# Down projection with paired products: four separate products in one row ahead of the last four groups

## The chip, the cores and the metric

The kernel runs on one core of a Trainium2 chip. The metric is the device time of one execution in microseconds (us). The engines are TensorE (PE, matrix products), VectorE (DVE), ScalarE (ACT), GpSimd (POOL) and SyncE (SP), which here only issues DMAs. Each engine runs its own instructions in order and waits for the others by semaphores.

## What is computed

A model of 256 tokens and width 2048: a gMLP block, a stick-breaking attention block, then a block with mLSTM and MoBA attention and an FFN. The change lies in that last FFN, all in fp32:

```
x2 = rmsnorm(x, norm_ffn_pre)
u  = square(relu(x2 @ w_up))        # 256x2048 @ 2048x8192
y  = u @ w_down                     # 256x8192 @ 8192x2048
x  = x + rmsnorm(y, norm_ffn_post)
```

## The kernel before, in words

**Three products for one.** A weight block is loaded to `stage`. ACT rounds it to a high half (`wh`, line 657), DVE makes the low half `wl` = block - `wh` (line 1173), and PE runs low x high, high x high and high x low in place of one fp32 product (lines 2125 to 2127). The tokens are split likewise into `yth` and `ytl`. The unit of the order is a *group*: one 512 KB weight load (256 x 512), split once, 12 matmuls for two token halves and two rows of 128. `home` (built at lines 255 to 262) lists all 935 groups in the order in which PE runs them. `wh` and `wl` hold 5 groups, so ACT splits group j once PE has ended group j - 5 (signal `used`). `where[...]` and `end(...)` give positions in this list.

**Order by slots.** Each engine's program is written out by hand. `slot(n)` in ACT's and DVE's programs means: first do all high (low) halves up to position n + 3; in SP's: first issue all loads whose buffer comes free up to n + 3. What stands behind a `slot` is done after that, in order.

**The FFN** runs in four quarters q of the hidden width. In each, `up` has four chunks c of 512 columns. ACT takes relu and square of a finished chunk (1122, 1125), DVE turns it (`turn_chunk`, 1234), SP moves it into `ytl` with four DMAs (479), ACT makes its high half (`up_high`, which calls `chunk_high`, 685) and DVE its low half (`chunk_low`, 1222). Then `down` multiplies these 2048 rows by four chunks of 512 output columns, summed in `dacc`.

**Pairs.** Two neighbouring chunks of `down`, (q, 0) with (q, 1) and (q, 2) with (q, 3), make a *pair*; there are 7, numbered 0 to 6 (at q = 3 only the first). For their first 512 rows, a 2 x 2 product of blocks is done with seven half products instead of eight, as in Strassen's and Winograd's method. A half product is a group of 6 matmuls (lines 2188 to 2190). P2, P3 and P4 are added into the banks of the pair's own chunks. The four *separate* products P1, P5, P6 and P7 each have a bank of their own, 4 to 7. The weights of a pair are four blocks, b11, b12, b21 and b22. P1 uses b11 itself. P5 uses t1 = b12 - b11 (line 1185), P6 uses t2 = b22 - t1 (1190), P7 uses t3 = b22 - b12 (1192), and P4 uses t4 = b21 - t1 (1195). DVE makes each of them in place, in `operand`, right behind the low half of the group before in the chain (t1 behind P1's, t2 behind P5's, t3 behind P6's), and ACT's high half of the product waits for it.

**The pair around PE.** The separate products stand in the list among the last four groups of the unit before the pair: at pairs 0, 2, 4 and 6 that unit is `up` (q, 3), at pairs 1, 3 and 5 it is the pair (q, 0), whose last four groups are k = 12 and 14 of both chunks. `apart` (ACT) copies P1's bank to SBUF (1101) and P5's bank to `rowb` (`fifth`, 1108). `together` (DVE) makes u2 = P6 + P1 (1957), u3 = P7 + u2 (1961), v = u2 + P5 (1963) and w = u3 + P5 (1965). `early` (DVE, 1974) adds the four results to `dacc` from q = 1 on. `down_evac` adds a finished chunk's banks.

For q = 2 the positions are: `up` (2, 3) begins at 822 and ends at 834 (`end`, the position behind its last group); P1 is 826.

Of the kernel before, what the change touches and what calls it, by code (L numbers as in the profile page):

```python
# [11 lines left out]
ALU = mybir.AluOpType  # L12
ACT = mybir.ActivationFunctionType
# [17 lines left out]
P1, P5, P6, P7, P2, P3, P4 = range(7)  # L31
# [105 lines left out]
def _program(nc, A, out, ctx):  # L137
    at = [((nc.sbuf_base + 511) // 512) * 512]

    def sb(name, shape, dt=F32, offset=None):  # L140
        size = int(np.prod(shape[1:])) * (2 if dt == BF16 else 4)
        where = at[0] if offset is None else offset
        if offset is None:
            at[0] += (size + 31) // 32 * 32
            assert at[0] <= nc.sbuf_usable_end, (name, at[0])
        t = nc.alloc_sbuf_tensor_at("t_" + name, shape, dt, offset=where)
        return t[tuple(slice(None) for _ in shape)], where
# [11 lines left out]
    rowb, _ = sb("rowb", [128, 2, 512])  # L159
# [33 lines left out]
    banks = [ctx.enter_context(nc.psum_tensor(f"bank{i}", [128, 512], F32))[:, :] for i in range(8)]  # L193
# [21 lines left out]
    used = signal("used")  # L215
# [7 lines left out]
    act = signal("act")  # L223
# [4 lines left out]
    vec = signal("vec")  # L228
# [6 lines left out]
    pairs = halved_pairs()  # L235
# [19 lines left out]
    home = []  # L255
    for u, (_, own) in enumerate(units):
        m = units[u + 1][0] if u + 1 < len(units) else None
        for n, group in enumerate(own):
            ahead = n - len(own) + 4
            if m is not None and ahead >= 0:  # L260
                home.append((m, ahead))
            home.append(group)
    N = len(home)
    where = {h: j for j, h in enumerate(home)}
    first = {chunk[0]: where[chunk[0], 4 if chunk[0] in pair_of else 0] for chunk in chunks}
# [51 lines left out]
    def end(*name):  # L317
        return max(j for j, (x, k) in enumerate(home) if x == name) + 1
# [16 lines left out]
    def cols(c):  # L335
        return slice(512 * c, 512 * c + 512)
# [35 lines left out]
    sum_l, sum_h = mtl[:, 0:4, :], mtl[:, 4:8, :]  # L372
    sum_raw = vreg[:, 4096:5120].rearrange("p (f s) -> p f s", f=4)
    added = vreg[:, 6144:8192].rearrange("p (f s) -> p f s", f=4)
    fifth = rowb[:, 0, :]

    def g8(j):
        return gsm[:, j, :]
# [194 lines left out]
    def gpsimd(e):  # L573
# [62 lines left out]
                e.tensor_tensor(h, h, d, ALU.add).then_inc(*pool("x3", c, i))  # L636

        for c in range(4):
            e.wait_ge(*(vec.at("dr", c - 2, 1) if c >= 2 else vec.at("w", "pair", len(pairs) - 1)))
            load_row(c, A["norm_ffn_post_2"][:, cols(c)], "ffn", c)  # L640


    def scalar(e):
# [16 lines left out]
        def slot(n):  # L660
            highs(n + 3)
# [423 lines left out]
                e.wait_ge(*(pool.at("x3", c, i) if c >= 2 else vec.at("x3", c, i)))  # L1085
                squares(hres[:, i, cols(c)], ssq2[:, i, c:c + 1], "x3", c, i)
        def up_high(q, c):
            slot(end("up", q, c) + 4)
            chunk_high(yth, ytl, c, 1.0, "up", q, c)
            if c == 0:  # L1090
                slot(end("up", q, c) + 5)
                e.wait_ge(*vec.at("sums", q))
                e.activation(sum_h, sum_raw, ACT.Copy).then_inc(*xhi("sums", q))

        def apart(m):

            slot(where[m, P1] + 1)
            e.wait_ge(*used.at(where[m, P1]))
            if m and pairs[m - 1][0][1]:
                e.wait_ge(*vec.at("early", m - 1, 0))  # L1100
            e.activation(quarters(m)[0], banks[4], ACT.Copy).then_inc(*act("first", m))
            slot(where[m, P5] + 1)
            e.wait_ge(*used.at(where[m, P5]))
            if m:
                e.wait_ge(*vec.at("w", "pair", m - 1))
            else:
                e.wait_ge(*vec.at("mixed", 2))
            e.activation(fifth, banks[5], ACT.Copy).then_inc(*act("fifth", m))

        e.wait_ge(*vec.at("sF"))  # L1110
        for q in range(4):
            for c in range(4):
# [48 lines left out]
    def vector(e):  # L1161
# [35 lines left out]
        def slot(n):  # L1197
            lows(n + 3)
# [142 lines left out]
        for p, n in ((0, 37), (1, 40)):  # L1341
# [3 lines left out]
            for q in (2 * p, 2 * p + 1):  # L1345
                w = wst[:, 4 * q:4 * q + 4, :]
# [24 lines left out]
        for h in range(2):  # L1371
            for c in range(4 * h, 4 * h + 4):
# [11 lines left out]
                for i in range(2):  # L1384
                    v = v_tile(c, i)
# [551 lines left out]
        def up_turn(q, c):  # L1937
            slot(end("up", q, c) + 1)
            e.wait_ge(*act.at("squared", q, c))
            turn_chunk(lambda i: buf[c % 2][:, i, :], flat[zt_buf[c]], "up", q, c)  # L1940
            slot(end("up", q, c) + 4)
            if c == 0:
                sums(q)
            chunk_low(yth, ytl, c, 1.0, "up", q, c)
            if c == 0:
                slot(end("up", q, c) + 6)
                e.wait_ge(*xhi.at("sums", q))
                e.tensor_tensor(sum_l, sum_raw, sum_h.bitcast(F32), ALU.subtract).then_inc(*xlo("sums", q))

        def together(m):  # L1950

            _, q, c = pairs[m][0]
            one, three_, two, four_ = quarters(m)
            slot(where[m, P6] + 1)
            e.wait_ge(*used.at(where[m, P6]))
            e.wait_ge(*act.at("first", m))
            e.tensor_tensor(two, banks[6], one, ALU.add).then_inc(*vec("u2", m))
            slot(where[m, P7] + 1)
            e.wait_ge(*used.at(where[m, P7]))
            e.wait_ge(*vec.at("u2", m))  # L1960
            e.tensor_tensor(three_, banks[7], two, ALU.add).then_inc(*vec("u3", m))
            e.wait_ge(*act.at("fifth", m))
            e.tensor_tensor(two, two, fifth, ALU.add).then_inc(*vec("v", "pair", m))
            e.wait_ge(*vec.at("u3", m))
            e.tensor_tensor(four_, three_, fifth, ALU.add).then_inc(*vec("w", "pair", m))

        def early(m):
            _, q, c = pairs[m][0]
            if q:
                slot(where[m, P7] + 3)  # L1970
                e.wait_ge(*vec.at("w", "pair", m))
                for n in range(2):
                    d = dacc[:, :, cols(c + n)]
                    e.tensor_tensor(d, d, added[:, 2 * n:2 * n + 2, :], ALU.add).then_inc(*vec("early", m, n))  # L1974

        def down_evac(q, c):
            slot(end("down", q, c))
            e.wait_ge(*used.at(end("down", q, c) - 1))
            if q == 3:
                e.wait_ge(*row_in[c % 2].at("ffn", c))  # L1980
            for i in range(2):
                d, p = dacc[:, i, cols(c)], accs("down", q, c)[i]
                e.tensor_tensor(d, d, p, ALU.add).then_inc(*vec("d", q, c, i))
                if q == 3:
                    e.wait_ge(*vec.at("d", 3, c, i))
                    e.tensor_tensor(buf[c][:, i, :], d, rowb[:, c % 2, :], ALU.mult).then_inc(*vec("dr", c, i))

        for q in range(4):
            for c in range(3):
                up_turn(q, c)  # L1990
            together(first_of["down", q, 0])
            up_turn(q, 3)
            early(first_of["down", q, 0])
            down_evac(q, 0)
            if ("down", q, 2) in first_of:
                together(first_of["down", q, 2])
            down_evac(q, 1)
            if ("down", q, 2) in first_of:
                early(first_of["down", q, 2])
            for c in range(2, 3 if q == 3 else 4):  # L2000
                down_evac(q, c)
# [115 lines left out]
    def tensor(e):  # L2117
        count = {"group": 0}
        free = {}
# [47 lines left out]
        def halved(m, f, j):  # L2167

            a, b = pairs[m]
            bank = {P1: banks[4], P5: banks[5], P6: banks[6], P7: banks[7], P2: accs(*a)[0], P3: accs(*b)[0],  # L2170
                    P4: accs(*a)[1]}[f]
            if f <= P7:
                bank_of(4 + f)
                free[4 + f] = (act.at("first", m), act.at("fifth", m), vec.at("u2", m), vec.at("u3", m))[f]
            if f in (P1, P2):
                e.wait_ge(*arrival(("down", a[1], 0), 0))
            elif f == P5:
                e.wait_ge(*xlo.at("sums", a[1]))
            for n in range(2):
                h, l = {P1: (tokens(yth, 2 * n, 0), tokens(ytl, 2 * n, 0)),  # L2180
                        P2: (tokens(yth, 2 * n + 1, 0), tokens(ytl, 2 * n + 1, 0)),
                        P4: (tokens(yth, 2 * n + 1, 1), tokens(ytl, 2 * n + 1, 1)),
                        P5: (tokens(sum_h, 0, n), tokens(sum_l, 0, n)),
                        P6: (tokens(sum_h, 1, n), tokens(sum_l, 1, n)),
                        P7: (tokens(sum_h, 2, n), tokens(sum_l, 2, n)),
                        P3: (tokens(sum_h, 3, n), tokens(sum_l, 3, n))}[f]
                w_h, w_l = wh[:, j % N_SPLIT, n, :], wl[:, j % N_SPLIT, n, :]
                e.matmul(bank, h, w_l, start=n == 0 and f <= P7, stop=False)  # L2188
                e.matmul(bank, h, w_h, start=False, stop=False)  # L2189
                last = e.matmul(bank, l, w_h, start=False, stop=n == 1 and f <= P7)  # L2190
            return last
# [361 lines left out]
```

## Time and profile before

| what | us |
|---|---|
| median of 3 runs | 2572.11 (2571.88 to 2573.97) |
| the profiled execution, its own time | 2571.94 |
| span of that execution, first to last instruction | 2570.2 |
| PE matmul busy | 2560.8 |
| DVE busy | 1674.4 |
| ACT busy | 1275.5 |
| POOL busy | 34.8 |

The times of one execution come from the hardware profiler. Busy time counts an engine's instructions; waits are not busy. PE's matmuls are pipelined and their ends are modelled, so that one record reaches over the start of the next. Lines (L1173) are lines of the kernel before. The FFN fills the stretch from about 1.87 ms to the end.

### The profile page before, as it was taken

The page shows a single profiled execution, that of the slowest core. Times are in us where ns is not written, and L with a number is a line of the kernel's source. Part 1 is how long each engine was busy: PE and PEld are TensorE (multiplying, and loading weights), DVE is VectorE, ACT ScalarE, POOL GpSimd, SP SyncE. Part 2 cuts the span into 40 slices and gives each one's busy share as a digit, 9 for nine tenths or more (in the row PEclk, how much of TensorE's full clock was granted, in tenths as well). Part 3 has the DMA queues.
Part 4 walks back from the last instruction along what each step waited for, and adds up shares of the span by engine and source line. Part 5 has one row for each costly group of instructions (what it writes and reads, how often), then busy time and mean ns, then how long its engine had stood idle before and what let it go on. Part 6 is the DMA issues. An engine that isn't in the chain of part 4 may idle for free.

```text
span 2570.2 us, 29334 instructions
## 1 busy us (share of the span) xinstructions
PE 2560.8 (100%) x11461; PEld 2122.5 (83%) x11461; DVE 1674.4 (65%) x1949; ACT 1275.5 (50%) x1534; POOL 34.8 (1%) x56
## 2 busy tenths in 40 slices
PE   9999999999999999999999999999999999999999
PEld 8888888888888888888888888888888888888887
DVE  5646565566666566676866876555577668577676
ACT  6554443444545555455444444444465455464453
POOL 1000000000000000000000000000020000000000
PEclk9999999999999999999999999999999999999999
DMA  8767776676777777777565777666666667666674
GB/s 284 205 185 209 208 204 194 198 206 198 215 217 199 212 202 202 219 228 221 162 195 168 217 219 211 201 201 196 220 181 217 214 189 219 199 208 226 194 216 148
DMA packets 534795, 527.43 MB, mean 205 GB/s; under 512 B 294896, under 2 KB 297824, under 8 KB 534656
## 3 DMA queue, kind: packets, MB, share of 16 engines
q1 hardware_dynamic: 531856, 518.09, 67.8%
q0 software_dynamic: 2384, 6.93, 1.1%
q8 instruction: 91, 1.49, 0.2%
q10 hardware_dynamic: 416, 0.52, 0.1%
q14 instruction: 48, 0.39, 0.0%
HBM read 488.24 MB, written 2.10 MB: 191 GB/s over the span
## 4 chain that ended last, share of the span: by engine, by line
PE 97%; DVE 1%; ACT 0%; DMA 0%; SPq 0%; issue 0%
PE bank L2125 31%; PE bank L2127 31%; PE bank L2126 31%; PE bank L2189 1%; PE bank L2190 1%; PE bank L2188 1%; PE bank L2307 1%; PE bank L2296 1%; PE bank L2286 1%; DMA t_ytl<-t_pool 0%; SPq L479 0%; DVE t_wl L1173 0%; DVE t_vreg L1974 0%; DVE t_pool L1234 0%; PE bank L2220 0%
## 5 line engine op out<-in xcount | busy, mean ns | idle before, releaser
L1173 DVE TENSOR_TENSOR t_wl<-t_stage,t_wh 128x1024 fp32r<-128x1024 f32 x850 | 1030.3, 1221 | 681.8 <-ACT t_wh L657 679.6
L657 ACT ACTIVATE t_wh<-t_stage 128x1024 fp32r<-128x1024 f32 x851 | 892.0, 1057 | 848.2 <-PE bank L2127 819.0
L2125 PE MATMUL bank<-t_wl,t_xth 128*128 128x512 f32 x2480 | 972.0, 392 | 0.5 <-DVE t_xtl L1215 0.5
L2127 PE MATMUL bank<-t_wh,t_xtl 128*128 128x512 f32 x2480 | 965.2, 389 | 0.0
L2126 PE MATMUL bank<-t_wh,t_xth 128*128 128x512 f32 x2480 | 965.0, 389 | 0.0
L2127 PEld LDWEIGHTS bank<-t_wh,t_xtl 128*128 128x128 f32 x2480 | 465.5, 188 | 97.0
L2125 PEld LDWEIGHTS bank<-t_wl,t_xth 128*128 128x128 f32 x2480 | 465.7, 188 | 96.6 <-DVE t_xtl L1215 0.9
L2126 PEld LDWEIGHTS bank<-t_wh,t_xth 128*128 128x128 f32 x2480 | 465.7, 188 | 95.9 <-issue 0.2
L2125 PE MATMUL bank<-t_wl,t_yth 128*128 128x512 f32 x914 | 356.0, 389 | 3.2 <-DVE t_wl L1173 3.2
L2127 PE MATMUL bank<-t_wh,t_ytl 128*128 128x512 f32 x914 | 355.2, 389 | 0.0
L2126 PE MATMUL bank<-t_wh,t_yth 128*128 128x512 f32 x914 | 355.2, 389 | 0.0
L2125 PEld LDWEIGHTS bank<-t_wl,t_yth 128*128 128x128 f32 x914 | 171.6, 188 | 39.7 <-DVE t_wl L1173 4.5
L2126 PEld LDWEIGHTS bank<-t_wh,t_yth 128*128 128x128 f32 x914 | 171.6, 188 | 35.5
L2127 PEld LDWEIGHTS bank<-t_wh,t_ytl 128*128 128x128 f32 x914 | 171.6, 188 | 35.4
L1173 DVE TENSOR_TENSOR t_wl<-t_ubuf,t_wh 128x1024 fp32r<-128x1024 f32 x83 | 101.4, 1223 | 41.3 <-ACT t_wh L657 41.0
L657 ACT ACTIVATE t_wh<-t_ubuf 128x1024 fp32r<-128x1024 f32 x83 | 87.7, 1057 | 76.1 <-PE bank L2127 63.2
L1234 DVE STREAM_TRANSPOSE t_pool<-t_pool 128x512 f32<-128x512 f32 x96 | 99.3, 1073 | 0.0
L685 ACT ACTIVATE t_yth<-t_ytl 128x1024 fp32r<-128x1024 f32 x32 | 33.9, 1061 | 77.5 <-DMA t_ytl<-t_pool 77.0
L1222 DVE SCALAR_TENSOR_TENSOR t_ytl<-t_ytl,t_yth 128x1024 fp32r<-128x1024 f32 x32 | 39.2, 1224 | 47.9 <-ACT t_yth L685 47.7
L2125 PE MATMUL bank<-t_wl,t_mth 128*128 128x512 f32 x128 | 49.9, 390 | 0.0
L2127 PE MATMUL bank<-t_wh,t_mtl 128*128 128x512 f32 x128 | 49.8, 389 | 0.0
L2126 PE MATMUL bank<-t_wh,t_mth 128*128 128x512 f32 x128 | 49.8, 389 | 0.0
(341 smaller groups left out, 1242.1 us busy)
## 6 DMA issues: line engine op xcount, KB each, us to landing
t_stage<-in_a_w_in_dram SPq DMA_DIRECT2D x192, 512.0 KB, 4.2
t_stage<-in_w_in_dram SPq DMA_DIRECT2D x178, 512.0 KB, 4.3
t_stage<-in_b_w_in_dram SPq DMA_DIRECT2D x128, 512.0 KB, 4.5
t_stage<-in_w_down_dram SPq DMA_DIRECT2D x91, 512.0 KB, 4.8
t_stage<-in_w_up_dram SPq DMA_DIRECT2D x88, 512.0 KB, 4.4
t_stage<-in_a_w_out_dram SPq DMA_DIRECT2D x64, 512.0 KB, 4.2
t_ubuf<-in_w_up_dram SPq DMA_DIRECT2D x40, 512.0 KB, 4.3
t_ubuf<-in_w_down_dram SPq DMA_DIRECT2D x37, 512.0 KB, 5.3
```

The costliest lines, as they stand in the source:

```text
L657: e.activation(wh[:, j % N_SPLIT], stage[s], ACT.Copy).then_inc(*hi(j))
L685: e.activation(xh[:, 4 * c:4 * c + 4, :], xl[:, 4 * c:4 * c + 4, :].bitcast(F32), ACT.Copy, scale=scale).then_inc(*xhi(*name))
L1173: e.tensor_tensor(low, src, high.bitcast(F32), ALU.subtract).then_inc(*lo(j))
L1222: e.scalar_tensor_tensor(out=low, in0=low.bitcast(F32), scalar=scale, in1=high.bitcast(F32), op0=ALU.mult, op1=ALU.subtract).then_inc(*xlo ...
L1234: e.transpose(turn_out(dst, i), turn_in(src(i))).then_inc(*turned(*name) if i else turned())
L2125: e.matmul(o, h, w_l, start=start, stop=False)
L2126: e.matmul(o, h, w_h, start=False, stop=False)
L2127: return e.matmul(o, l, w_h, start=False, stop=stop)
L2188: e.matmul(bank, h, w_l, start=n == 0 and f <= P7, stop=False)
L2189: e.matmul(bank, h, w_h, start=False, stop=False)
L2190: last = e.matmul(bank, l, w_h, start=False, stop=n == 1 and f <= P7)
L2286: last = e.matmul(t[:, part], wst[:, 2 * c + j, :], v_tile(c, i)[:, part], start=True, stop=True)
```

## The change

The four separate products stand in one row ahead of the last four groups, not one ahead of each. For q = 2 the two orders are, by position:

```
        826  827  828  829  830  831  832  833
before  P1   k8   P5   k10  P6   k12  P7   k14
after   P1   P5   P6   P7   k8   k10  k12  k14
```

With it: the split of the last chunk of `up` (high and low half) moves from 4 to 8 groups behind the end of `up`; P5 stays in its bank until `w` is made, and the copy `fifth` is gone; and the four gain rows for the last norm, loaded on POOL's queue, wait for an earlier event.

```diff
@@ home @@
         for n, group in enumerate(own):
-            ahead = n - len(own) + 4
-            if m is not None and ahead >= 0:
-                home.append((m, ahead))
+            if m is not None and n == len(own) - 4:
+                home += [(m, f) for f in range(4)]
             home.append(group)
@@ gpsimd @@
         for c in range(4):
-            e.wait_ge(*(vec.at("dr", c - 2, 1) if c >= 2 else vec.at("w", "pair", len(pairs) - 1)))
+            e.wait_ge(*(vec.at("mixed", 2 + c) if c < 2 else vec.at("dr", c - 2, 1)))
             load_row(c, A["norm_ffn_post_2"][:, cols(c)], "ffn", c)
@@ scalar @@
         def up_high(q, c):
-            slot(end("up", q, c) + 4)
+            slot(end("up", q, c) + (8 if c == 3 else 4))
             chunk_high(yth, ytl, c, 1.0, "up", q, c)
...
             e.activation(quarters(m)[0], banks[4], ACT.Copy).then_inc(*act("first", m))
-            slot(where[m, P5] + 1)
-            e.wait_ge(*used.at(where[m, P5]))
-            if m:
-                e.wait_ge(*vec.at("w", "pair", m - 1))
-            else:
-                e.wait_ge(*vec.at("mixed", 2))
-            e.activation(fifth, banks[5], ACT.Copy).then_inc(*act("fifth", m))
@@ vector @@
             turn_chunk(lambda i: buf[c % 2][:, i, :], flat[zt_buf[c]], "up", q, c)
-            slot(end("up", q, c) + 4)
+
+        def up_low(q, c):
+            slot(end("up", q, c) + (8 if c == 3 else 4))
             if c == 0:
                 sums(q)
             chunk_low(yth, ytl, c, 1.0, "up", q, c)
...
-            e.wait_ge(*act.at("fifth", m))
-            e.tensor_tensor(two, two, fifth, ALU.add).then_inc(*vec("v", "pair", m))
+            e.tensor_tensor(two, banks[5], two, ALU.add).then_inc(*vec("v", "pair", m))
             e.wait_ge(*vec.at("u3", m))
-            e.tensor_tensor(four_, three_, fifth, ALU.add).then_inc(*vec("w", "pair", m))
+            e.tensor_tensor(four_, banks[5], three_, ALU.add).then_inc(*vec("w", "pair", m))
...
         for q in range(4):
             for c in range(3):
                 up_turn(q, c)
+                up_low(q, c)
             together(first_of["down", q, 0])
             up_turn(q, 3)
             early(first_of["down", q, 0])
+            up_low(q, 3)
             down_evac(q, 0)
@@ halved (PE) @@
-                free[4 + f] = (act.at("first", m), act.at("fifth", m), vec.at("u2", m), vec.at("u3", m))[f]
+                free[4 + f] = (act.at("first", m), vec.at("w", "pair", m), vec.at("u2", m), vec.at("u3", m))[f]
```

## Rows read from the trace of the kernel before

**Rows 1.** The page: busy us (share) xinstructions of each engine.
```profile
PE 2560.8 (100%) x11461; PEld 2122.5 (83%) x11461; DVE 1674.4 (65%) x1949; ACT 1275.5 (50%) x1534; POOL 34.8 (1%) x56
```
**Rows 2.** Waits of PE, 1790 to 2570 us: us in total, times, longest.
```profile
PE bank L2125 <- DVE t_wl L1173: 3.2, 3, 1.4
```
**Rows 3.** Chain that ended last: start, us, engine, tile, line.
```profile
2312.49 2.01 DVE t_pool L1234 x2
...
2317.49 3.17 DMA t_ytl<-t_pool
...
2323.01 2.27 DVE t_vreg L1974 x2
2325.28 1.15 DVE t_wl L1173
```
**Rows 4.** Timeline of PE: start, us, engine, line, operation [idle before <-releaser].
```profile
2326.47 0.50 PE L2125 MATMUL bank<-t_wl,t_yth 128*128 128x512 f32 x1 [0.91 <-DVE t_wl L1173]
2326.80 0.39 PE L2126 MATMUL bank<-t_wh,t_yth 128*128 128x512 f32 x1
```
**Rows 5.** Timeline of PE, P1 of pair 4 and the group behind it.
```profile
2291.39 0.39 PE L2188 MATMUL bank<-t_wl,t_yth 128*128 128x512 f32 x1
...
2292.76 0.39 PE L2125 MATMUL bank<-t_wl,t_xth 128*128 128x512 f32 x1
```
**Rows 6.** Timeline of DVE, 2283 to 2303 us.
```profile
2285.38 1.23 DVE L1185 TENSOR_TENSOR t_stage<-t_ubuf,t_stage 128x1024 f32<-128x1024 f32 x1
2286.53 2.07 DVE L1234 STREAM_TRANSPOSE t_pool<-t_pool 128x512 f32<-128x512 f32 x2
2288.52 1.19 DVE L1173 TENSOR_TENSOR t_wl<-t_ubuf,t_wh 128x1024 fp32r<-128x1024 f32 x1
2289.62 1.22 DVE L1173 TENSOR_TENSOR t_wl<-t_stage,t_wh 128x1024 fp32r<-128x1024 f32 x1
2290.94 1.23 DVE L1190 TENSOR_TENSOR t_stage<-t_stage 128x1024 f32<-128x1024 f32 x1
...
2295.59 1.23 DVE L1222 SCALAR_TENSOR_TENSOR t_ytl<-t_ytl,t_yth 128x1024 fp32r<-128x1024 f32 x1 [2.28 <-ACT t_yth L685]
2296.73 1.22 DVE L1173 TENSOR_TENSOR t_wl<-t_stage,t_wh 128x1024 fp32r<-128x1024 f32 x1
```
**Rows 7.** Timeline of ACT, 2282 to 2303 us.
```profile
2286.64 1.06 ACT L657 ACTIVATE t_wh<-t_stage 128x1024 fp32r<-128x1024 f32 x1 [1.67 <-DVE t_stage L1185]
...
2294.50 1.06 ACT L685 ACTIVATE t_yth<-t_ytl 128x1024 fp32r<-128x1024 f32 x1 [4.50 <-DMA t_ytl<-t_pool]
```
**Rows 8.** Timeline of PE, first matmul of P4 of pair 4.
```profile
2318.59 0.39 PE L2188 MATMUL bank<-t_wl,t_yth 128*128 128x512 f32 x1
```
**Rows 9.** Timeline of DVE at q = 3, first low half behind the turning.
```profile
2461.09 1.19 DVE L1173 TENSOR_TENSOR t_wl<-t_stage,t_wh 128x1024 fp32r<-128x1024 f32 x1
```
**Rows 10.** Timeline of PE at q = 3, first matmul of P1.
```profile
2463.97 0.39 PE L2188 MATMUL bank<-t_wl,t_yth 128*128 128x512 f32 x1
```
**Rows 11.** Timeline of DVE, low half of P1 of pair 1.
```profile
1981.52 1.22 DVE L1173 TENSOR_TENSOR t_wl<-t_ubuf,t_wh 128x1024 fp32r<-128x1024 f32 x1
```
**Rows 12.** Timeline of PE, first matmul of P1 of pair 1.
```profile
1989.66 0.39 PE L2188 MATMUL bank<-t_wl,t_yth 128*128 128x512 f32 x1
```
**Rows 13.** Groups by line and shape, 1900 to 2560 us | busy us, mean ns.
```profile
L1961 DVE TENSOR_TENSOR t_vreg<-bank,t_vreg 128x512 f32<-128x512 f32 x7 | 4.8, 683 | 0.0
L1963 DVE TENSOR_TENSOR t_vreg<-t_vreg,t_rowb 128x512 f32<-128x512 f32 x7 | 4.8, 681 | 0.0
L1108 ACT ACTIVATE t_rowb<-bank 128x512 f32<-128x512 f32 x7 | 4.1, 586 | 0.7 <-PE bank L2190 0.7
```
**Rows 14.** Timeline of SP's DMA issues, first load behind the chunk's four.
```profile
2318.21 0.78 SPq L466 DMA_DIRECT2D t_stage<-in_w_down_dram  x1
```
**Rows 15.** The page: DMA issues, count, KB each, median us to landing.
```profile
t_stage<-in_w_down_dram SPq DMA_DIRECT2D x91, 512.0 KB, 4.8
```
**Rows 16.** Stretches: us, busy of PE (x) and PEld (x) ..., PEclk, DMA.
```profile
2320.00:2340.00 20.00, 19.09 (x85) 15.47 (x84) 17.47 (x15) 11.53 (x12) 0.00 (x0) 1.00 0.62 210
```

More of the change, by code:

```diff
@@ L374, in _program @@
     added = vreg[:, 6144:8192].rearrange("p (f s) -> p f s", f=4)
-    fifth = rowb[:, 0, :]
     def g8(j):
```

## The prediction

> **What bounds the kernel now.** I read the page's busy table first: TensorE (PE) is busy for 2560.8 of 2570.2 us [rows 1]. No change of order can take more than some 9 us from that, while a new hole in PE's work adds in full. So the question is only which holes the change closes and which it opens. Next I read PE's waits. In the changed stretch they are for the low halves of weights that VectorE (DVE) makes: three times, 3.2 us in sum [rows 2]. The chain of waits shows where they come from, here for the third quarter of the FFN (q = 2): DVE turns the last activation chunk (L1234), its 4 DMAs are issued and land (3.17 us), ScalarE (ACT) splits it, DVE makes its low half (L1222), then adds a finished pair to the sum (L1974, 2.27 us), and only then makes the weights that PE waits for [rows 3]. ACT and DVE run their programs in order, so the wait for that DMA holds every weight split queued behind it. The chain has the same steps at q = 1 and q = 3 (three times in all), and not at q = 0, which has no addition. The wait shown is too small: the record of the matmul before it lasts 0.39 us where the next was due after 0.227, and the first matmul behind it runs 0.33 instead of 0.227 to the next [rows 4], so each hole is 0.27 us longer than its record. That makes 3.2 + 3 x 0.27 = 4.0; with the first matmuls behind a hole some hundredths apart, I take 4.1 us lost.
>
> Last I read how far ahead the weights are made. The six matmuls of a separate product take 1.36 us (2291.39 to 2292.76) [rows 5], the twelve of a full group twice that, 2.72. Each group needs a high half from ACT (1.06 us) and a low half from DVE (1.22 us), and P5, P6 and P7 first need a weight combination from DVE (1.23 us) [rows 6, 7].
>
> **The change part by part.** *The last chunk's split moves back by four groups* (`up_high`, `up_low` for c = 3: from 4 to 8 groups behind the end of `up`). ACT and DVE first split weights up to 11 places behind that end, and only then wait for the DMA, which has landed by then. PE needs this chunk at the groups k = 12 of `down`, 15 places behind the end (11 at q = 3), so nothing waits for it. The addition L1974 now follows the turning at once: the turning ends at 2312.49 + 2.01 = 2314.50, the addition's 2.27 us bring DVE to 2316.77, the low half of P4's weights ends at 2317.99, and 0.2 us later (as at the hole, below) PE can use it, 2318.2 against P4's first matmul at 2318.59 [rows 3, 8]. 0.4 us are left; all three holes close: **-4.1 us**.
>
> *The row at the end of `up`* (pairs 0, 2, 4, 6). PE now runs P1, P5, P6, P7 1.36 us apart, where they were 4.08 apart. Their weights are a chain, each combination needs the one before, and DVE turns a chunk in the middle of it. I walk q = 2. P1's matmuls start at 2291.39, so P5 is due at 2292.75, P6 at 2294.11, P7 at 2295.47 and the next full group at 2296.83 [rows 5]. The combination for P5 (L1185) and the turning stay where they are, and ACT's high half of P5 takes the place at 2286.64 that it had [rows 6, 7]. DVE is free at 2288.52, and then, with hand-overs of 0.03 us between ACT and DVE and 0.10 from a low half to the combination behind it (2285.38 + 1.23 = 2286.61 to 2286.64; 2289.62 + 1.22 = 2290.84 to 2290.94) [rows 6, 7]: low half of P5 to 2289.70, combination for P6 2289.80 to 2291.03, ACT's high half 2291.06 to 2292.12, low half 2292.15 to 2293.37. At the hole of before DVE's low half ended at 2326.4 (2325.28 + 1.15) and PE ran as if started at 2326.6 (2326.80 less 0.227) [rows 3, 4]: I take 0.2 us from a low half to its use. P6 is usable at 2293.6, 0.5 before it is due. The combination for P7 starts right behind the low half (2293.29) and ends at 2294.51, ACT's high half at 2295.60, the low half at 2296.85: usable at 2297.05 where 2295.47 was due, **1.58 us** of hole. P7 then ends at 2298.41. Behind P7's weights DVE has the low half of chunk c = 2 (L1222, 1.14 us from its start to the next) [rows 6] and then the next full group's, which ends at 2299.13 and is usable at 2299.33: another **0.92**. The group after that is usable by 2300.5 and due at 2302.05, so it ends there: 2.50 us. The chunk's DMA released ACT at 2294.50 [rows 7], before ACT now comes to it (2295.5), so it adds nothing. DVE's first low half behind the turning is 2.87 us ahead of P1 at q = 2 (2288.52, 2291.39) and 2.88 at q = 3 [rows 5, 6, 9, 10], so the four cases are alike: 4 x 2.50 = **+10.0 us**. The trace of before does not show this chain back to back. Its bounds are 0 (hidden as now) and 4 x 3.5 = 14 with 0.1 us more at each of ten hand-overs; I take the walk, since each of its steps has a row.
>
> *The row inside `down`* (pairs 1, 3, 5). ACT is released for P1's high half when PE ends the fifth group before it, 10.7 us ahead of P1; nothing holds it there any more. From the release: high half 1.1, low half 1.25, combination 1.3, chunk's low half 1.1, low half of P5 1.2, then combination, high and low half for P6 3.7 and for P7 3.5, and 0.2 to the use: 13.3 us, where P7 is due after 10.7 + 4.1 = 14.8. Were P1's low half made as late as now (1981.52, 8.1 us ahead of P1 at 1989.66) [rows 11, 12], the 12.2 us from its start would end when P7 is due (8.1 + 4.1 = 12.2). Room of 1.5 us by the one, of none by the other, no hole by either: **0 us**.
>
> *The fifth product's copy.* Seven copies of 586 ns leave ACT, and the adds that make `v` and `w` read bank 5 instead of SBUF. An add that reads a bank takes 683 ns, one that reads SBUF alone 681 [rows 13], and PE comes to the next P5 far behind `w`: 0 us. The Trainium skill (Perfetto Trace Analysis, Optimizing Scalar/DVE Operations) gives DVE about 65 ns more of access overhead on PSUM than on SBUF; for 14 adds that is an estimated 0.9 us of DVE beside PE's work, and the rows do not bear it out.
>
> *Loads and rows of gains.* The stage buffers rotate otherwise. The tightest load is the second block of a pair inside `down`: SyncE issues it behind the chunk's DMAs (2318.21), it lands 4.8 us later (median) at 2323.0, and the combination that needs it comes 2.5 us behind the release of P1 (2322.8), at 2325.3 [rows 14, 15]: 0 us, with 2.3 to spare. POOL's gain rows of `norm_ffn_post` start earlier and nothing waits for them.
>
> **Sum.** 2571.94 (the profiled execution's own time) + 10.0 - 4.1 = 2577.8. The median of the runs is 0.17 above it, so **2578.0 us**, 0.23% slower.
>
> **Rivals.** *The row is hidden after all* (faster): if DVE's turning came behind the combinations instead of ahead of them, 2.0 us would leave the chain and only the closed holes would count: 2572.1 - 4.1 = 2568.0. For it: DVE and ACT are idle for 2.28 and 4.5 us right behind this stretch [rows 6, 7]. Against: the turning is released before the low half of P5 is. It decides if P7's weights come 1.6 us earlier than walked. 12%. *The holes stay*: the addition right behind the turning leaves 0.4 us at P4; if the low half there is 1.8 us late at each of the three, the gain is given back: 2582.1. 10%. *Only P7 is late*: if the next group's low half got ahead of the chunk's, 4 x 1.58 - 4.1 = +2.2, so 2574.3. Against: the program has the chunk first. 10%. *It does not do what it says*: neither the gain nor the loss, 2572.1; for an error of mine in the order. 7%. *PE's clock falls in the new holes.* It was granted at 1.00, 2.4 GHz, across a stretch with a hole [rows 16]; the new ones are no longer than 1.6 us. At 1.2 GHz each full group would cost another 2.72 us; one in each quarter makes 10.9 more, 2588.9. 1%. The Trainium skill (TensorE: Matmul & The Clock Gate, What's actually happening) says that an idle array falls to 1.2 GHz. By that rule, were the new holes enough, 2588.9 would be the time; the row across a hole speaks against it.
>
> **How the numbers follow.** Forecast 60%: 2578.0, by itself 2576.5 to 2580. Range 2574.0 to 2582.3: forecast, holes that stay and the single late P7, 80%. A measurement here can tell about 0.2% (5.1 us) from no change, so slower begins at 2577.3. Faster 12%. Slower: holes stay 10, clock 1, and 49 of the forecast's 60, 60% in all. Same: the rest, 28%.
>
> **What would show it.** Right: eight waits of PE for L1173, in four twins, about 1.3 us by the record at P7 and 0.6 at the full group behind it, and no wait any more at the end of the chain over L685 and L1974; ACT's high halves of P6 and P7 released by the combinations. Wrong: a P6 that waits (the chain is longer than walked), a wait behind P4 (the addition), a wait at pairs 1, 3, 5, or a PE without waits (the first rival).

## The result and the profile after

| | before | after |
|---|---|---|
| median of 8 runs each, on one chip | 2572.84 us (2571.88 to 2576.45) | 2579.65 us (2579.10 to 2582.49) |
| profiled execution, its span | 2571.94, 2570.2 us | 2579.10, 2577.4 us |
| ratio of the times | | 1.0025, 95% interval 1.0016 to 1.0034 |

The change makes the kernel slower by 0.25%; the forecast was 2578.0 us. The busy table hardly moves against [rows 1]: TensorE (PE) runs the same 11461 matmuls. Of the 7.2 us between the profiled executions 2.1 stand in the table as busy time, because the records of matmuls around a hole are longer (last section); the holes below account for the rest and for these.

```profile
PE 2562.9 (99%) x11461; PEld 2121.7 (82%) x11461; DVE 1675.3 (65%) x1949; ACT 1273.3 (49%) x1527; POOL 34.8 (1%) x56
```

PE's waits in the FFN, the view of [rows 2] (us in total, times, longest). L2181 is a separate product, L2118 a full group, L1163 the low half of a weight (L1173 in before):

```profile
PE bank L2181 <- DVE t_wl L1163: 5.2, 4, 1.3
PE bank L2118 <- DVE t_wl L1163: 2.5, 4, 0.6
```

The three waits of before are gone; four pairs of new ones are there. All sit at the ends of the four `up` stretches. PE's timeline at q = 2 shows one pair. The last matmul of P6, the first two and the last of P7, and the first of the next full group:

```profile
2300.35 0.39 PE L2183 MATMUL bank<-t_wh,t_mtl 128*128 128x512 f32 x1
2302.03 0.50 PE L2181 MATMUL bank<-t_wl,t_mtl 128*128 128x512 f32 x1 [1.29 <-DVE t_wl L1163]
2302.37 0.40 PE L2182 MATMUL bank<-t_wh,t_mtl 128*128 128x512 f32 x1
...
2303.30 0.39 PE L2183 MATMUL bank<-t_wh,t_mtl 128*128 128x512 f32 x1
2304.30 0.50 PE L2118 MATMUL bank<-t_wl,t_xth 128*128 128x512 f32 x1 [0.62 <-DVE t_wl L1163]
```

I measure a hole by what it does to the schedule: how much longer than 1.36 us (separate product) or 2.72 us (full group) a group takes up to its last matmul. The four P7 lose 1.61, 1.59, 1.59 and 1.59 us, the four full groups behind them 0.95, 0.95, 0.95 and 0.91, and one group of the chunk (2, 3) 0.22: 10.36 us. The holes of before, measured in the same way, were 1.17, 1.22 and 1.71: 4.10 us. The FFN is thus 6.26 us longer.

The other 1.1 us arose at 55 us into the run (two matmuls start 1.23 us apart there, where 0.23 is the rule, and the next 0.34 later), in code that the change doesn't touch. In the profile of after ACT waits just before that for a load of weights; in a second profile of the same kernel (below) it waits for that load no more, and the FFN is reached at 1863.98 us, as in before (1864.06). That part is chance.

```profile
50.34 1.06 ACT L655 ACTIVATE t_wh<-t_stage 128x1024 fp32r<-128x1024 f32 x1 [5.37 <-DMA t_stage<-in_a_w_in_dram]
```

DVE's timeline shows the chain that made these holes (L1175, L1180, L1182: the combinations for P5, P6, P7; L1224 the turning; L1212 the chunk's low half). It answers to [rows 6].

```profile
2290.49 1.23 DVE L1175 TENSOR_TENSOR t_stage<-t_stage 128x1024 f32<-128x1024 f32 x1
2291.63 2.07 DVE L1224 STREAM_TRANSPOSE t_pool<-t_pool 128x512 f32<-128x512 f32 x2
2293.62 1.19 DVE L1163 TENSOR_TENSOR t_wl<-t_stage,t_wh 128x1024 fp32r<-128x1024 f32 x1
2294.91 1.23 DVE L1180 TENSOR_TENSOR t_stage<-t_stage 128x1024 f32<-128x1024 f32 x1
2297.26 1.23 DVE L1163 TENSOR_TENSOR t_wl<-t_stage,t_wh 128x1024 fp32r<-128x1024 f32 x1 [1.12 <-ACT t_wh L655]
2298.40 1.22 DVE L1182 TENSOR_TENSOR t_stage<-t_stage 128x1024 f32<-128x1024 f32 x1
2300.75 1.23 DVE L1163 TENSOR_TENSOR t_wl<-t_stage,t_wh 128x1024 fp32r<-128x1024 f32 x1 [1.13 <-ACT t_wh L655]
2301.89 1.22 DVE L1212 SCALAR_TENSOR_TENSOR t_ytl<-t_ytl,t_yth 128x1024 fp32r<-128x1024 f32 x1
```

The two bracketed idle times are the mark of a chain: DVE does nothing for 1.1 us, waiting for the high half that ACT makes from DVE's own combination. From the first low half to the next is 3.6 us, and to the third 3.5; PE takes 1.36 us for each product. ACT's side is the mirror image, and no DMA holds it (in [rows 7] one did, for 4.50 us):

```profile
2296.17 1.06 ACT L655 ACTIVATE t_wh<-t_stage 128x1024 fp32r<-128x1024 f32 x1 [3.36 <-DVE t_stage L1180]
2299.66 1.06 ACT L655 ACTIVATE t_wh<-t_stage 128x1024 fp32r<-128x1024 f32 x1 [2.43 <-DVE t_stage L1182]
2300.62 1.04 ACT L683 ACTIVATE t_yth<-t_ytl 128x1024 fp32r<-128x1024 f32 x1
```

### The profile page after: what moved, and what is told of

It reads as the page before. It is cut to its first block, busy times and chain, and to the rows that moved or that the text cites. A ratio compares the mean times of both kernels' runs of the same rounds, so it can differ in the third digit from the quotient of the medians.

```text
span 2577.4 us, 29320 instructions
## 1 busy us (share of the span) xinstructions
PE 2562.9 (99%) x11461; PEld 2121.7 (82%) x11461; DVE 1675.3 (65%) x1949; ACT 1273.3 (49%) x1527; POOL 34.8 (1%) x56
## 4 chain that ended last, share of the span: by engine, by line
PE 96%; DVE 2%; ACT 1%; DMA 1%; issue 0%; DVEq 0%; ACTq 0%
PE bank L2118 30%; PE bank L2119 30%; PE bank L2120 30%; DVE t_wl L1163 1%; PE bank L2300 1%; PE bank L2289 1%; DMA t_stage<-in_a_w_in_dram 1%; PE bank L2183 1%; PE bank L2182 1%; PE bank L2181 1%; ACT t_wh L655 1%; PE bank L2279 1%; DVE t_pool L1224 0%; ACT t_pool L1112 0%; DVE t_stage L1180 0%
## 5 line engine op out<-in xcount | busy, mean ns | idle before, releaser
L1163 DVE TENSOR_TENSOR t_wl<-t_stage,t_wh 128x1024 fp32r<-128x1024 f32 x856 | 1037.6, 1222 | 709.5 <-ACT t_wh L655 707.0
L2118 PE MATMUL bank<-t_wl,t_xth 128*128 128x512 f32 x2480 | 972.7, 392 | 3.7 <-DVE t_wl L1163 2.5
L2118 PEld LDWEIGHTS bank<-t_wl,t_xth 128*128 128x128 f32 x2480 | 465.6, 188 | 102.1 <-DVE t_wl L1163 4.2
L2118 PE MATMUL bank<-t_wl,t_yth 128*128 128x512 f32 x914 | 355.7, 389 | 0.0
L2118 PEld LDWEIGHTS bank<-t_wl,t_yth 128*128 128x128 f32 x914 | 171.6, 188 | 35.8 <-DVE t_vreg L1974 0.3
L1163 DVE TENSOR_TENSOR t_wl<-t_ubuf,t_wh 128x1024 fp32r<-128x1024 f32 x77 | 93.9, 1221 | 44.2 <-ACT t_wh L655 43.9
L655 ACT ACTIVATE t_wh<-t_ubuf 128x1024 fp32r<-128x1024 f32 x77 | 81.3, 1056 | 66.1 <-PE bank L2120 54.2
L1224 DVE STREAM_TRANSPOSE t_pool<-t_pool 128x512 f32<-128x512 f32 x96 | 99.3, 1073 | 0.0
L1212 DVE SCALAR_TENSOR_TENSOR t_ytl<-t_ytl,t_yth 128x1024 fp32r<-128x1024 f32 x32 | 39.1, 1223 | 23.5 <-ACT t_yth L683 23.1
L2118 PE MATMUL bank<-t_wl,t_mth 128*128 128x512 f32 x128 | 49.9, 390 | 0.0
```

What stands on the lines that cost most here:

```text
L655: e.activation(wh[:, j % N_SPLIT], stage[s], ACT.Copy).then_inc(*hi(j))
L1163: e.tensor_tensor(low, src, high.bitcast(F32), ALU.subtract).then_inc(*lo(j))
L1212: e.scalar_tensor_tensor(out=low, in0=low.bitcast(F32), scalar=scale, in1=high.bitcast(F32), op0=ALU.mult, op1=ALU.subtract).then_inc(*xlo ...
L1224: e.transpose(turn_out(dst, i), turn_in(src(i))).then_inc(*turned(*name) if i else turned())
L2118: e.matmul(o, h, w_l, start=start, stop=False)
```

## The experiments

Theory: the change is two opposite parts. The late split of the last chunk closes three holes (-4.1 us); the row at the end of `up` opens eight (+10.0); the row inside `down` and the copy of the fifth product cost nothing. Rivals: the turning, 2.0 us of DVE's time, is what makes P7 late; a part that I priced at nothing costs something. Each kernel was timed beside the kernel before on the same chip; "hole" has the meaning given above.

### The late split alone

The kernel before, with only the last chunk's split moved.

```diff
         def up_high(q, c):
-            slot(end("up", q, c) + 4)
+            slot(end("up", q, c) + (8 if c == 3 else 4))
...
             together(first_of["down", q, 0])
             up_turn(q, 3)
             early(first_of["down", q, 0])
+            up_low(q, 3)
```

> The order of the groups is that of before; only the last chunk's split is moved (both halves from 4 to 8 groups behind the end of up, and the addition L1974 ahead of the low half). My theory: the three holes of before (1.17, 1.22 and 1.71 us) come from the DMA wait of that split and the addition behind it, so they close and nothing opens: 4.1 us less than before, ratio 0.9984, and PE has no wait for low halves in the FFN. Rival: the addition, now right behind the turning, opens holes of its own at P4, or the holes had another cause: ratio 1.000.

Measured: 2568.01 us (2567.55 to 2569.87), ratio 0.9982, interval 0.9973 to 0.9990. The profiled executions differ by 4.3 us (2567.65 to 2571.94). Of the waits of PE in the FFN only two that both kernels have are left, and ACT comes to the chunk without waiting for its DMA:

```profile
PE bank L2129 <- DVE t_xtl L1215: 0.4, 1, 0.4
PE bank L2500 <- ACT t_cpb L1150: 0.4, 1, 0.4
```

```profile
2321.46 1.06 ACT L657 ACTIVATE t_wh<-t_ubuf 128x1024 fp32r<-128x1024 f32 x1 [1.66 <-PE bank L2131]
2322.43 1.04 ACT L685 ACTIVATE t_yth<-t_ytl 128x1024 fp32r<-128x1024 f32 x1
```

The -4.1 us are there: from its first matmul to its last group the FFN takes 694.07 us in this trace and 698.14 in before. The addition right behind the turning makes no wait at P4. The medians are 5.2 us apart (2573.23 to 2568.01); the profiled execution of before is 1.3 us under the median of that series, and what its slower executions lose no trace shows. The same kernel once more, on another chip; "the run above" in its expectation is the one with the bank add put first (below):

> The late split of the last chunk alone, once more beside the run above on the same chip. My theory: no hole in the FFN in this execution either, and the same time as the run above within 0.5 us. Rival: chance landings open holes here too.

Measured: 2567.96 us, ratio 0.9980, interval 0.9971 to 0.9989. Its FFN takes 694.07 us again, without a new hole, and it is 0.2 us from the run beside it.

### The row alone

The changed kernel with the last chunk's split put back to where it was.

```diff
-            slot(end("up", q, c) + (8 if c == 3 else 4))
+            slot(end("up", q, c) + 4)
...
             up_turn(q, 3)
-            early(first_of["down", q, 0])
             up_low(q, 3)
+            early(first_of["down", q, 0])
```

> The changed kernel with the last chunk's split put back to 4 groups behind the end of up, ahead of the addition: the row of four products alone. My theory: the two parts add up. The row costs 4 x 2.54 = 10.2 us and the holes of 4.1 us are back as in before, so 10.2 us more than before, ratio 1.0040. Rival: the row itself frees DVE early (together is done before the turning), so that the old holes close even without the move of the split: 6 us more than before, ratio 1.0024.

Measured: 2589.58 us (2588.28 to 2589.95), ratio 1.0060, interval 1.0047 to 1.0072. The loss is 16 us, where the theory had 10.

```profile
PE bank L2181 <- DVE t_wl L1163: 8.6, 6, 1.7
PE bank L2118 <- DVE t_vreg L1974: 3.9, 3, 1.6
PE bank L2118 <- DVE t_wl L1163: 3.2, 6, 0.6
```

The row at the end of `up` costs what it should (1.58 to 1.60 and 0.91 to 0.94 at each, 10.0 us). The old three holes shrank to 0.42, 0.71 and 0.73. But two P7 inside `down` lose 1.97 and 1.99 us now, and 5.05 us are lost at the first groups of the chunks (q, 3), where PE waits for a bank that L1974 (`down_evac`) has yet to add up. In sum 20.96 - 4.10 = 16.9; the profiled executions differ by 16.3. ACT's and DVE's timelines at the pair inside `down` of q = 1 show why:

```profile
2154.35 1.06 ACT L683 ACTIVATE t_yth<-t_ytl 128x1024 fp32r<-128x1024 f32 x1 [4.03 <-DMA t_ytl<-t_pool]
```

```profile
2162.26 1.22 DVE L1163 TENSOR_TENSOR t_wl<-t_stage,t_wh 128x1024 fp32r<-128x1024 f32 x1
...
2173.10 1.23 DVE L1163 TENSOR_TENSOR t_wl<-t_stage,t_wh 128x1024 fp32r<-128x1024 f32 x1 [1.12 <-ACT t_wh L655]
```

With the early split ACT again waits 4.03 us for the chunk's DMA, and DVE is still behind by this and by the addition when it comes to P1's low half (2162.26, 6.2 us ahead of P1). The chain to the end of P7's low half takes 12.1 us from there, and P7 is due 10.3 after it. In before the lead at this pair was the same 6.2 us:

```profile
2156.04 1.22 DVE L1173 TENSOR_TENSOR t_wl<-t_stage,t_wh 128x1024 fp32r<-128x1024 f32 x1
```

```profile
2162.20 0.39 PE L2188 MATMUL bank<-t_wl,t_yth 128*128 128x512 f32 x1
```

At pair 5 it was 6.2 as well. The 8.1 of [rows 11, 12] are those of pair 1, at q = 0, where nothing is added to `dacc`; there the row alone has 8.2 and its P7 doesn't wait. So the parts don't add: at pairs 3 and 5 the row is free at its P7 only because the late split makes room for it (the lead at pair 3 is 9.5 us in after).

### The changed kernel again

> The changed kernel itself once more. My theory: its FFN holds 10.2 us of holes at the four rows against 4.1 in before, so 6.1 to 6.4 more than before; the first 1.86 ms are the same program, and the further 1.1 us that its first profile spent at the third chunk of v was chance: this profile reaches the FFN at the time of the others (1863.7 to 1864.2 us), ratio 1.0024 to 1.0026. Rival: the changed kernel is slower ahead of the FFN as well: again 1865.1 us there.

Measured: 2579.31 us (2578.51 to 2581.96), ratio 1.0024, interval 1.0015 to 1.0033.

```profile
PE bank L2181 <- DVE t_wl L1163: 5.2, 4, 1.3
PE bank L2118 <- DVE t_wl L1163: 2.5, 4, 0.6
PE bank L2118 <- DVE t_vreg L1974: 1.1, 2, 0.6
```

The eight holes at `up` are the same to 0.04 us. New is the third line: the groups that wait for L1974 lose 0.15, 0.93 and 0.77 us, where the first profile had 0.22 in one place. This term varies between the two profiles, 0.2 and 1.9 us, and the FFN is 6.3 and 7.9 us longer than before.

### The second cause split off: the row inside `down` only

The row stands only where the preceding unit is itself a pair's (pairs 1, 3, 5); at the ends of `up` the order is that of before. The late split is in.

```diff
-            if m is not None and n == len(own) - 4:
+            inside = m is not None and units[u][0] is not None
+            if inside and n == len(own) - 4:
                 home += [(m, f) for f in range(4)]
+            if m is not None and not inside and n >= len(own) - 4:
+                home.append((m, n - len(own) + 4))
```

> The changed kernel with the row only at pairs 1, 3 and 5 (inside down); at the end of up the four products are interleaved as before. My theory: the rows inside down cost nothing but up to 0.3 us at the start of chunk (q, 3), and the late split closes the old holes: 3.9 us less than before, ratio 0.9985. Rival: the rows inside down cost part of what the changed kernel lost: ratio 0.999 or more.

Measured: 2569.74 us (2567.95 to 2570.61), ratio 0.9984, interval 0.9975 to 0.9993. The ratio is the expected one, the working was not: 0.3 us were expected to be lost, and 2.3 are. No P7 waits; three first groups of the chunks (q, 3) lose 0.33, 0.89 and 1.06 us behind the bank adds (L1977 here). In DVE's timeline the four adds of the pair's products (L1952 to L1959), all due at once now that the products end together, stand with two low halves in front of the bank add:

```profile
2175.99 0.68 DVE L1952 TENSOR_TENSOR t_vreg<-bank,t_vreg 128x512 f32<-128x512 f32 x1
2176.78 0.69 DVE L1956 TENSOR_TENSOR t_vreg<-bank,t_vreg 128x512 f32<-128x512 f32 x1
2177.39 0.68 DVE L1957 TENSOR_TENSOR t_vreg<-bank,t_vreg 128x512 f32<-128x512 f32 x1
2177.99 0.68 DVE L1959 TENSOR_TENSOR t_vreg<-bank,t_vreg 128x512 f32<-128x512 f32 x1
2178.58 1.21 DVE L1166 TENSOR_TENSOR t_wl<-t_stage,t_wh 128x1024 fp32r<-128x1024 f32 x1
2179.72 1.22 DVE L1166 TENSOR_TENSOR t_wl<-t_ubuf,t_wh 128x1024 fp32r<-128x1024 f32 x1
2180.85 1.28 DVE L1977 TENSOR_TENSOR t_vreg<-t_vreg,bank 128x512 f32<-128x512 f32 x2
```

In before the first of the four (L1957) stands 4 us ahead of the other three, between two low halves. If the four adds are the cause, the bank add put ahead of them must close these holes:

```diff
             down_evac(q, 0)
-            if ("down", q, 2) in first_of:
-                together(first_of["down", q, 2])
             down_evac(q, 1)
             if ("down", q, 2) in first_of:
+                together(first_of["down", q, 2])
                 early(first_of["down", q, 2])
```

> The kernel of row_down_only with DVE's four adds of the pair (together) moved behind the adds that empty the banks of chunk (q, 1). My theory: the holes of 0.33, 0.89 and 1.06 us at the first group of chunk (q, 3) are PE waiting for that chunk's banks, emptied late because the four adds (2.4 us) stand ahead and DVE came late to them behind a weight load that landed late; with the adds behind, they close: no wait for the banks, about 2 us less than row_down_only, ratio 0.9982 as the late split alone. Rival: PE waits there because low halves and loads are late as such; moving the adds only shifts the hole: ratio as row_down_only, 0.9984 or more.

Measured: 2567.77 us (2567.36 to 2570.14), ratio 0.9976, interval 0.9967 to 0.9986. The bank add now starts 3.1 us earlier, and PE waits for no bank in the whole FFN (0.09 us are left at one group). The medians are 2.0 us apart, though taken on two chips. Luck with the loads is not the reason: ahead of this stretch ACT waits 2.12 and 1.21 us for two loads of weights, where it was 2.21 and 1.35 in the run above. DVE's timeline now:

```profile
2177.72 1.27 DVE L1977 TENSOR_TENSOR t_vreg<-t_vreg,bank 128x512 f32<-128x512 f32 x2
2178.92 0.68 DVE L1952 TENSOR_TENSOR t_vreg<-bank,t_vreg 128x512 f32<-128x512 f32 x1
```

### The chain: without the combinations

The changed kernel without the three combinations of a pair: P5 and P6 take one loaded block, P7 another, so the three products are of other weights.

```diff
-            if f == P1:
...
-                e.tensor_tensor(t1, t3, t1, ALU.subtract).then_inc(*vec("t1", m))
-            elif f == P5:
...
-                e.tensor_tensor(t1, t22, t1, ALU.subtract).then_inc(*vec("t2", m))
-            elif f == P6:
-                e.tensor_tensor(t3, t22, t3, ALU.subtract).then_inc(*vec("t3", m))
-            elif f == P2:
+            if f == P2:
```

> The changed kernel without the weight combinations t1, t2 and t3: P5 and P6 take b11 itself, P7 takes b12, so DVE leaves out 3 of 4 subtractions in each pair and ACT's high halves wait for loads alone. My theory: the holes at P7 come from the serial chain of combination, high half and low half; without the combinations ACT and DVE are four groups ahead as elsewhere and all holes go: 4.1 us less than before, ratio 0.9984. Rival: the cause is the rate of splits, four weight splits in 5.4 us of PE, or PE's own switching between banks in the row: holes stay, ratio above 1.001.

Measured: 2567.44 us (2567.11 to 2567.67), ratio 0.9976, interval 0.9966 to 0.9986. All new holes are gone, those at `up` and those behind the bank adds. DVE still turns the chunk in the same place, and the low half behind it need not wait for ACT:

```profile
2283.97 2.06 DVE L1212 STREAM_TRANSPOSE t_pool<-t_pool 128x512 f32<-128x512 f32 x2
2285.96 2.32 DVE L1163 TENSOR_TENSOR t_wl<-t_stage,t_wh 128x1024 fp32r<-128x1024 f32 x2
```

The row of four products costs PE nothing by itself; the chain of combinations does. Three combinations take 3.7 us of DVE, and two of them bring 1.1 us of waiting for ACT each (the brackets above); this run removes both together, so it doesn't say which half decides.

### The chunk's low half in the way

The split of chunk c = 2 also goes 8 groups behind its end.

```diff
-            slot(end("up", q, c) + (8 if c == 3 else 4))
+            slot(end("up", q, c) + (8 if c >= 2 else 4))
```

> The changed kernel with the split of chunk c = 2 also moved from 4 to 8 groups behind the end of its up chunk, so that DVE makes the low half of the full group behind P7 before the chunk's. My theory: the second hole of each twin (0.95 us) is DVE's time for the chunk's low half and goes, the first (1.59 at P7) stays: 3.8 us less than the changed kernel, 2.5 us more than before, ratio 1.0010. Rival: the second hole follows from P7 being late, whatever DVE does between: no change against the changed kernel, ratio 1.0026.

Measured: 2576.55 us (2574.96 to 2577.86), ratio 1.0011, interval 1.0002 to 1.0020.

```profile
PE bank L2181 <- DVE t_wl L1163: 5.2, 4, 1.3
PE bank L2118 <- DVE t_vreg L1974: 1.8, 3, 0.8
```

P7 loses the same (1.58, 1.63, 1.60, 1.59), and the hole behind it is gone at all four places. So the second hole of each pair, 3.8 us in sum, is the chunk's low half (L1212) standing ahead of the next group's weights, as walked. Against this the groups behind the bank adds lose 2.7 us, which the expectation left out; whether the moved split adds to them or chance does, one profile can't say.

### The turning in the way

The turning of chunk c = 2 moves from 1 to 6 groups behind its end, its DMAs from 1 to 7, its split from 4 to 10, behind the copy of P1 (ACT) and the pair's four adds (DVE).

```diff
         def up_turn(q, c):
-            slot(end("up", q, c) + 1)
+            slot(end("up", q, c) + (6 if c == 2 else 1))
...
         def up_high(q, c):
-            slot(end("up", q, c) + (8 if c == 3 else 4))
+            slot(end("up", q, c) + (4, 4, 10, 8)[c])
```

> The changed kernel with DVE's turning of chunk c = 2 moved behind the weights of the row and of two groups more (from 1 to 6 groups behind the end of its up chunk; its DMAs from 1 to 7, its split from 4 to 10). Rival, as in my prediction: the turning's 2.0 us leave the chain, P7 is 1.6 us earlier, and all eight holes close: 4.1 us less than before, ratio 0.9984. My theory now: ACT makes P5's high half beside the turning, so only 0.8 us of it lie in the chain: four holes of 0.8 us stay at P7, those behind it go as the chunk's low half no longer stands there: 3.2 - 4.1, about 0.7 us less than before, ratio 0.9997.

Measured: 2584.83 us (2583.79 to 2586.21), ratio 1.0044, interval 1.0032 to 1.0057. In total this was a miss by some 12 us. At the disputed place it still tells the two apart: the four P7 lose 0.84, 0.86, 0.86 and 0.84 us, not 1.6 and not 0. The turning lasts 2.0 us, and taking it away gives 0.75, since ACT makes the high half of P5 beside it:

```profile
2291.73 1.23 DVE L1176 TENSOR_TENSOR t_stage<-t_stage 128x1024 f32<-128x1024 f32 x1
2294.08 1.23 DVE L1164 TENSOR_TENSOR t_wl<-t_stage,t_wh 128x1024 fp32r<-128x1024 f32 x1 [1.13 <-ACT t_wh L655]
```

Between these two DVE waits for ACT, where the turning stood. What was gained there was lost further on: the chunk's DMA is issued later, ACT waits 5.75 us for it, and behind ACT's wait stands the emptying of banks (L1113).

```profile
PE bank L2184 <- DVE t_wl L1164: 7.0, 7, 1.6
PE bank L2121 <- ACT t_pool L1113: 3.7, 4, 1.2
PE bank L2121 <- DVE t_vreg L1975: 1.3, 3, 0.6
```

```profile
2315.72 1.06 ACT L683 ACTIVATE t_yth<-t_ytl 128x1024 fp32r<-128x1024 f32 x1 [5.75 <-DMA t_ytl<-t_pool]
```

The first groups of (q, 1) lose 4.92 us, three P4 5.63, and the groups behind the bank adds 2.23. I priced none of the three. That the P4 are late by the same wait of ACT is what I take from the order of the work; no run shows it apart.

### The copy of the fifth product

The late split alone, and P5 read from its bank, without the copy.

```diff
-            e.activation(fifth, banks[5], ACT.Copy).then_inc(*act("fifth", m))
...
-            e.tensor_tensor(two, two, fifth, ALU.add).then_inc(*vec("v", "pair", m))
+            e.tensor_tensor(two, banks[5], two, ALU.add).then_inc(*vec("v", "pair", m))
```

> The order of before with the late split of the last chunk, and P5 read from its bank with ACT's copy left away: the two parts of the change without the row. My theory: the copy is worth nothing, so the time is that of the late split alone, 5.2 us less than before as measured (4.1 by its holes), ratio 0.9982 to 0.9984. Rival: adds that read two banks or ACT's freed time move it by over 1 us either way.

Measured: 2567.76 us (2567.41 to 2570.17), ratio 0.9981, interval 0.9972 to 0.9990; the late split alone had 0.9982 and 0.9980. In the FFN the copy is worth nothing: 694.07 us from first matmul to last group with it and without it. Behind the last group something small is left: from its last matmul to the end of the span the three profiles with the copy take 8.0 us, all nine without it 7.7. ACT comes to its last instruction that much earlier; why, no run shows.

## Why the prediction was right

- *The late split, -4.1 us.* Right. The holes of before are 4.10 us by the ends of the groups, and they go. 0.4 us were forecast to be left at P4. DVE's timeline of after has the first low half behind the addition start at 2324.26, so it ends at 2325.4 to 2325.5; P4's first matmul is at 2326.24, and with 0.2 us to the use 0.5 to 0.6 are left:

```profile
2322.02 2.33 DVE L1965 TENSOR_TENSOR t_vreg<-t_vreg 128x1024 f32<-128x1024 f32 x2
2324.26 3.50 DVE L1163 TENSOR_TENSOR t_wl<-t_stage,t_wh 128x1024 fp32r<-128x1024 f32 x3
```

- *The row at the end of `up`, +10.0 us.* Right in its size and in its parts: 1.58 forecast and 1.59 to 1.61 measured at P7, 0.92 and 0.91 to 0.95 behind it, 10.1 in sum. The working was right for the right reason: without the combinations all holes go, without the chunk's low half the second of each pair, without the turning half of the first. I had bounded this term by 0 and 14 and taken the walk; the hand-overs of 0.03 and 0.10 us, read where the engines' records met in before, held back to back.
- *The row inside `down`, 0 us.* This term was mis-sized. Its P7 had the room forecast (1.3 us measured, 1.5 forecast). But I asked only when the weights would be there, and not what else DVE has to do for PE in this stretch: the four adds of the products moved together in front of the bank add that frees PE's next bank. That costs 0.2 and 1.9 us in the two profiles of the changed kernel, and 2.3 with the row inside `down` only; with the bank add first it costs 0.1. My other working was wrong in its lead. "As late as now" was read at pair 1, with 8.1 us; at pairs 3 and 5 it was 6.2 in before, and by 12.2 - (6.2 + 4.1) this working would have given 1.9 us of hole at each. With the late split taken away 1.97 and 1.99 were measured. So even the forecast of 0 us at P7 holds only together with the late split, which the sum, as two parts that add, doesn't say.
- *The copy, 0 us.* Right. The Trainium skill (Perfetto Trace Analysis, Optimizing Scalar/DVE Operations) would have made each add that now reads a bank some 65 ns longer. No run here shows that: the adds of `v` (L1954) and `w` (L1956) in after read bank 5 and take 681 ns, those of before read SBUF and take 681 and 683 [rows 13 have the first].

```profile
L1956 DVE TENSOR_TENSOR t_vreg<-bank,t_vreg 128x512 f32<-128x512 f32 x7 | 4.8, 681 | 0.0
L1954 DVE TENSOR_TENSOR t_vreg<-bank,t_vreg 128x512 f32<-128x512 f32 x7 | 4.8, 681 | 0.0
```

- *The sum.* Forecast +5.9 us. The medians are 6.8 apart, the profiled executions 7.2: 6.26 in the FFN, 1.1 by a late load at the start that has nothing to do with the change, and 0.3 less behind the FFN. That the total fell within 2 us is in part luck: the changed kernel's medians are 11.3 to 11.7 us above those of the late split alone, where 10.0 were forecast, and the late split's are 5.2 to 6.2 below those of before, where 4.1 were. The two misses take each other back.
- *The rivals.* "Only P7 is late" fell with the order of the program: the chunk's low half does stand first, and it took moving it to get this case (2576.55; it had 2574.3, without the bank waits, 2.7 us in that run). "The row is hidden after all" had a wrong price: I let the turning take its full 2.0 us out of the chain, and it takes 0.75, so P7's 1.6 us could never have closed by it. "The holes stay" fell with the 0.5 to 0.6 us at P4. The clock stayed at 1.00, 2.4 GHz, across both holes (stretch, busy time of PE, PEld, DVE, ACT and POOL, granted clock, DMA share, GB/s); the rule by which it would have been 2588.9 did not come into play at holes of this length.

```profile
2286.00:2306.00 20.00, 18.09 (x79) 14.33 (x78) 14.39 (x13) 10.96 (x13) 0.00 (x0) 1.00 0.36 89
```

**What is faster than both.** The late split without the row: 2568.0 us in two series, 0.2% under the kernel before. With the copy gone, or with the row inside `down` and the bank add first, it is the same (2567.8 each). By their traces PE has no hole left but the two waits of 0.4 us, one at the FFN's first matmuls and one in the norm behind it, so another order of the same matmuls has nothing to win between them.

## What to carry to other kernels

Before work that needs prepared operands is put closer together, divide: the time of the chain that prepares one (here 3.5 us for combination, high and low half, with the hand-overs) by the time that PE takes for it (1.36 us). Where the chain is longer, keep other work between, however idle the two engines look. Take the lead with which it starts from each place that the change touches: here it was 8.1 us at one pair and 6.2 at two others. When an engine that runs in order waits for a DMA, count everything that is queued behind the wait, and put the waiting instruction where the DMA has landed; and for each stretch list all that the helping engine owes to PE, the emptying of banks as well as the weights.

## What the runs showed of the hardware

- The record of a wait of PE is too small by 0.3 us for each: 1.29 in the record was 1.59 in the schedule, 0.62 was 0.95. The matmul ahead of the hole is recorded for 0.39 us where the next is due after 0.23, and the first behind it takes 0.34 to its successor. I had this from one hole of 0.9 us in before; it holds for eight more of two lengths.
- Two profiles of one program differ by 1 to 2 us in single places, and both times ACT waits for a load: the one at 50 us (1.1 us), and the one ahead of the bank waits that were 0.2 and 1.9 us. In the second profile of the changed kernel ACT waits 1.98 us for a load of weights there, where it was 0.53 in the first, and the low halves behind it come later. That this makes the bank waits longer is read from the order of the work, not tested:

```profile
2175.51 1.06 ACT L655 ACTIVATE t_wh<-t_ubuf 128x1024 fp32r<-128x1024 f32 x1 [1.98 <-DMA t_ubuf<-in_w_down_dram]
```
